# The first modulation of a two-layer transformer kernel: condition vector loaded first and turned alone, first four weight blocks split along the contraction

## The chip, the cores and the metric

The kernel runs on one core of one Trainium2 chip. The time is the device time of one execution, in microseconds (us); all numbers of a trace are counted from the start of its span. Engines are named as the profile names them: PE (TensorE), PEld (its weight loads), DVE (VectorE), ACT (ScalarE), POOL (GpSimd), SP (SyncE, which here only issues DMAs).

## The reference, cut to what matters

```
def reference(x, c, rel_bias, ada_w, ada_b, norm_attn, ...):       # x (1,512,1024), c (1,1024), all float32
    c_act = jax.nn.silu(c)
    for layer in range(2):
        mod = c_act @ ada_w[layer] + ada_b[layer]                    # ada_w[layer] (1024, 6144)
        sh_a, sc_a, g_a, sh_f, sc_f, g_f = jnp.split(mod, 6, axis=-1)
        h = modulate(rmsnorm(x, norm_attn[layer]), sh_a, sc_a)       # h * (1 + sc_a) + sh_a
        y = diff_attention(h, ...) if layer == 0 else dilated_attention(h, ...)
        x = x + g_a[:, None, :] * y
        h = modulate(rmsnorm(x, norm_ffn[layer]), sh_f, sc_f)
        x = x + g_f[:, None, :] * hier_moe(h, ...)
    return x
```

What matters here is the very first thing that layer 0 needs: `sh_a` and `sc_a`, the first 2048 columns of `c_act @ ada_w[0] + ada_b[0]`, and the normalised `x`, from which the modulated `h` is made for the first projections.

## The kernel before

Layer 0 is: setup, modulation, projections with attention between them, output projection, routing, then 32 experts whose weights are streamed; layer 1 the same with another attention. Each engine has its own instruction list in `program`, written out by hand, and the lists meet through semaphores. The order on an engine is the order of its code, and a waiting instruction holds all that stands behind it.

**Weights.** SP loads weights into a `ring` of six slots of 2 MB (`load`, L449, and L486 for the key and query weights, two halves of 1 MB) in the order that `block_order` gives: modulation blocks 0 to 3 ("mod 0" to "mod 3" below, slots 0 to 3), key and query weights of the first heads ("kq 0", slot 4), value weights ("v 0", slot 5), mod 4, 5, 6, kq 1, and so on. A slot is loaded again when its user is done (`used`). A modulation block before is 512 columns of `ada_w` with all 1024 rows, 8 pieces of 2 KB in each of 128 partitions. Tokens `x` come by a DMA of POOL (L558, 4 KB rows), followed on its queue by six small loads (L566). The constants and the small vectors come by ACT's DMAs (L684 to L702): constants, then `c`, norm gains and biases into rows of `W`, then the buckets of the position bias.

**Setup.** PE turns the vectors into columns (`colV` with 57 columns, `c` among them, L1607; `colA`, the modulation bias, L1608). DVE copies them from PSUM (L1020, L1026), scales a few and forms the sums for the mixing weight (L1028, L1030). ACT takes the Silu of `c` (L704) and the Exp for the mixing weight (L707), each with a table load. DVE spreads the result over 32 equal columns (L1033), so that PE can use it as weights. Two matmuls make the table of the position bias (L1611, L1612); DVE copies it (L1042, L1043), POOL writes it to DRAM (L568) and reads it back as a band matrix into `V` (L572, "hankel", which waits for kq 0 too).

**Norm.** ACT squares the four token chunks with a running sum (L732) and takes roots (L716); DVE normalises them into `XN` (L1052, L1056, L1060) and signals `xn_ready`.

**The first modulation.** For each of mod 0 to 3, PE multiplies the block (L1636): its four 32-column parts of the array work side by side on four of the eight contraction chunks, twice, so the 512 results stand in four partial sums of 32 equal rows. ACT copies them (L746); `mod_reduce` sums them over the partitions and turns them into a column, 4 matmuls with one column each (L1624); DVE adds the bias (`mod_columns`, L1100). After the fourth, DVE makes the scales (L1071) and signals `mod_ready`.

**The turn.** PE turns the normalised tokens, 8 groups of 4 transposes (L1670), into banks 2 to 5; ACT (L750, even groups) and DVE (L1115, odd groups) apply scale and shift while they copy to `HT`. A bank is used again when it has been copied.

**Projections.** `unit(n)`, 24 of them (L1695), two PSUM banks in turn. Unit 0 is the key of head 0, unit 1 its query. Behind unit 1 PE makes the bias tables (L1765, waits for the hankel DMA) and the reduction of mod 4 (L1624, again `mod_reduce`). From mod 4 on, DVE forms the modulation itself (`sum_part`, L1078 and L1080, 8 instructions for a block); in its list mod 4 stands ahead of copying out unit 0 (L1130), for which unit 2 waits.

Of the kernel before, what the change touches and what calls it, by code (L numbers as in the profile page):

```python
# [10 lines left out]
ALU = mybir.AluOpType  # L11
# [4 lines left out]
P = 128  # L16
# [25 lines left out]
C_KCOL, C_NCOL, C_SEL, C_END = 772, 773, 774, 810  # L42
# [3 lines left out]
V_C, V_NA, V_KN, V_KAB = 0, 8, 24, 32  # L46
V_QG, V_KG, V_SUB, V_BQ, V_BK = 48, 49, 50, 51, 54
V_END = 57
# [121 lines left out]
def constants():  # L170
# [14 lines left out]
    c[:, C_32] = 1 / 32  # L185
# [40 lines left out]
def program(nc, t, const, masks, buckets, out):  # L226
    with ExitStack() as ctx:
# [85 lines left out]
        t1_in, t1_pe, t1_copy = sem("t1_in"), sem("t1_pe"), sem("t1_copy")  # L313

# [106 lines left out]
        def _(sp):  # L421
# [129 lines left out]
            sp.wait_ge(out_done, 16 * TC)  # L551
# [130 lines left out]
        def _(act):  # L682

            act.dma_start(C[:, :], const).then_inc(const_in, 16)  # L684
            vecs = [(V_C, t["c"].rearrange("b (k p) -> (b k) p", p=P)),
                    (V_NA, t["norm_attn"].rearrange("l (k p) -> (l k) p", p=P)),
# [16 lines left out]
            act.wait_ge(setup_dve, 1)  # L703
            act.activation(cact[:, :], colV[:, V_C:V_C + KC], ACT.Silu).then_inc(setup_act, 1)  # L704

            act.wait_ge(setup_dve, 3)
            act.activation(lamw[:, 2:4], lamw[:, 0:2], ACT.Exp).then_inc(setup_act, 1)  # L707

            for l in range(LAYERS):
# [31 lines left out]
                if l == 0:  # L741
                    for i in range(4):
                        act.wait_ge(mod_pe, i + 1)
                        if i >= 2:
                            act.wait_ge(mod_red, i - 1)
                        act.activation(ACC[i % 2], bank[4 + i % 2], ACT.Identity).then_inc(mod_part, 1)  # L746
                    act.wait_ge(mod_ready, 1)
                    for k in range(0, KC, 2):
                        act.wait_ge(*s["xt_pe"](k + 1))
                        act.activation(ht3[:, k, :], bank[2 + k % 4], ACT.Identity,  # L750
                                       bias=mod[:, k:k + 1], scale=scl[:, 0, k:k + 1]).then_inc(s["ht_ready"].sem, 2)
# [51 lines left out]
                    act.add_instruction(mybir.InstLoadActFuncSet(name=nc.get_next_instruction_name(), act_func_set_id=LN_EXP_SET))  # L803
                    for n in range(UNITS0 + 6):
# [155 lines left out]
                if l == 0:  # L960
                    act.wait_ge(t1_pe, 1)
# [54 lines left out]
        def _(dve):  # L1016
            step = Steps(dve, dve_s)

            dve.wait_ge(setup_pe, 1)
            dve.tensor_copy(colV[:, :], bank[0][:, 0:V_END]).then_inc(setup_dve, 1)  # L1020
            dve.wait_ge(setup_dve, 1)
            step(dve.tensor_scalar(colV[:, V_QG:V_QG + 1], colV[:, V_QG:V_QG + 1], DH ** -0.5, None, ALU.mult))
            step(dve.tensor_scalar(colV[:, V_BQ:V_BQ + GROUPS], colV[:, V_BQ:V_BQ + GROUPS], DH ** -0.5, None, ALU.mult))
            step(dve.tensor_scalar(colV[:, V_SUB:V_SUB + 1], colV[:, V_SUB:V_SUB + 1], 1 - LAM_INIT, None, ALU.mult))
            dve.wait_ge(setup_pe, 2)
            dve.tensor_copy(colA[:, :], bank[1][:, 0:96]).then_inc(setup_dve, 1)  # L1026
            lp = W[:, 256:512].rearrange("p (a i n) -> p a i n", a=2, i=2)
# [7 lines left out]
            dve.wait_ge(setup_act, 2)  # L1035
            step(dve.tensor_tensor(lamw[:, 4:5], lamw[:, 3:4], lamw[:, 2:3], ALU.subtract))
            step(dve.tensor_scalar(nlam[:, :], lamw[:, 4:5], LAM_INIT, None, ALU.subtract))

            dve.wait_ge(bias_in, 32)
            dve.memset(V[BUCKETS:BUCKETS + 1, 4096 + FALL:4096 + FALL + H], NEG).then_inc(setup_dve, 1)  # L1040
            dve.wait_ge(setup_pe, 3)
            step(dve.tensor_copy(W[0:H, 0:512], bank[2][0:H, :]))  # L1042
            dve.tensor_copy(W[0:H, 512:512 + 3 * P], bank[3][0:H, 0:3 * P]).then_inc(setup_dve, 1)  # L1043

            for l in range(LAYERS):
# [60 lines left out]
                if l == 0:  # L1106
                    norm(s["ss_ready"], s["rms_arg"], s["rms_root"], s["xn_ready"])
                    for i in range(4):
                        mod_columns(i)
# [3 lines left out]
                    for k in range(1, KC, 2):  # L1113
                        dve.wait_ge(*s["xt_pe"](k + 1))
                        dve.tensor_scalar(ht3[:, k, :], bank[2 + k % 4], scl[:, 0, k:k + 1], mod[:, k:k + 1], ALU.mult, ALU.add).then_inc(q_ht, 1)  # L1115
# [487 lines left out]
        def _(pe):  # L1603

            pe.wait_ge(const_in, 16)
# [8 lines left out]
            def mod_reduce(i):  # L1614

                acc = ACC[i % 2]
                if i < 4:
                    pe.wait_ge(mod_part, i + 1)
                else:
                    pe.wait_ge(mod_sum, i - 3)  # L1620
                pe.wait_ge(mod_col, i)
                for j in range(4):
                    by_two = slice(2 * P * (j // 2) + j % 2, 2 * P * (j // 2 + 1), 2)
                    ins = pe.matmul(bank[6][:, 4 * i + j:4 * i + j + 1], acc[:, by_two if 6 <= i < 10 else slice(j * P, (j + 1) * P)],  # L1624
                                    C[:, C_32:C_32 + 1] if i < 4 else ones[:, 0:1], start=True, stop=True)
# [656 lines left out]
```

## Time and profile before

| | us |
|---|---|
| three runs | 1897.32, 1898.48, 1899.91; median 1898.48 |
| the profiled execution, device time | 1904.66 |
| its span in the trace | 1902.9 |
| PE busy | 1518.0 (80%) |
| DVE, ACT, POOL busy | 514.1, 371.6, 91.6 |
| DMA moved | 548.02 MB, mean 288 GB/s |

The page shows the span in 40 slices of 47.6 us with the busy share of each engine in tenths, and the chain of work that ended last by engine and line. The other views used are: the chain in order of time; the waits of one engine; the timeline (start, duration, line, shape, count, and in brackets the idle time of the engine before it with what ended it); windows (busy time of each engine in a stretch, and the granted clock of TensorE); and the DMA queues in a window. q1 is SP's queue, q10 ACT's, q0 POOL's.

### The profile page before, as it was taken

The page shows a single profiled execution, that of the slowest core. Times are in us where ns is not written, and L with a number is a line of the kernel's source. Part 1 is how long each engine was busy: PE and PEld are TensorE (multiplying, and loading weights), DVE is VectorE, ACT ScalarE, POOL GpSimd, SP SyncE. Part 2 cuts the span into 40 slices and gives each one's busy share as a digit, 9 for nine tenths or more (in the row PEclk, how much of TensorE's full clock was granted, in tenths as well). Part 3 has the DMA queues.
Part 4 walks back from the last instruction along what each step waited for, and adds up shares of the span by engine and source line. Part 5 has one row for each costly group of instructions (what it writes and reads, how often), then busy time and mean ns, then how long its engine had stood idle before and what let it go on. Part 6 is the DMA issues. An engine that isn't in the chain of part 4 may idle for free.

```text
span 1902.9 us, 16563 instructions
## 1 busy us (share of the span) xinstructions
PE 1518.0 (80%) x6360; PEld 671.8 (35%) x6360; DVE 514.1 (27%) x1178; ACT 371.6 (20%) x916; POOL 91.6 (5%) x99
## 2 busy tenths in 40 slices
PE   5999998997867757683698999998887756847845
PEld 2455554443222222231344455543432212312311
DVE  2675554340000000010576122225500100100103
ACT  3133344311101100110310234342210100101100
POOL 1000001010000000000000000002000000000000
PEclk9999998999878888897799999999998978978977
DMA  9972523389999999999766021021599999999996
GB/s 346 360 283 76 190 89 136 127 320 382 410 410 401 408 410 392 404 410 400 262 221 221 0 85 48 26 108 56 223 409 409 410 409 409 410 404 404 410 404 236
DMA packets 183413, 548.02 MB, mean 288 GB/s; under 512 B 8940, under 2 KB 46301, under 8 KB 182302
## 3 DMA queue, kind: packets, MB, share of 16 engines
q1 hardware_dynamic: 153536, 492.85, 66.5%
q0 software_dynamic: 12384, 36.41, 5.0%
q10 hardware_dynamic: 17406, 17.59, 2.9%
q8 instruction: 56, 0.92, 0.2%
q14 instruction: 31, 0.25, 0.0%
HBM read 530.37 MB, written 28.34 MB: 294 GB/s over the span
## 4 chain that ended last, share of the span: by engine, by line
PE 55%; DMA 27%; SPq 10%; DVE 5%; issue 2%; ACT 1%; DVEq 0%
PE psum L2144 12%; DMA ring<-in_moe_w_up_dram 11%; SPq L449 9%; PE psum L1897 9%; PE psum L1695 9%; DMA ring<-in_moe_w_down_dram 7%; PE psum L2177 5%; DMA ring<-in_moe_w_gate_dram 5%; PE psum L1867 3%; PE psum L1750 3%; DVE W L1080 1%; DMA T<-in_moe_w_up_dram 1%; DMA XN<-in_moe_w_up_dram 1%; DMA ring<-in_ada_w_dram 1%; PE psum L1724 1%
## 5 line engine op out<-in xcount | busy, mean ns | idle before, releaser
L2144 PE MATMUL psum<-ring,V 128*32 128x512 f32 (+2 forms) x1712 | 440.1, 677 | 182.1 <-DMA ring<-in_moe_w_up_dram 77.5
L2144 PEld LDWEIGHTS psum<-ring,V 128*32 128x32 f32 (+2 forms) x1712 | 145.2, 146 | 415.0 <-issue 408.5
L2177 PE MATMUL psum<-ring,V 128*32 128x512 f32 (+2 forms) x768 | 199.4, 661 | 74.0 <-DMA ring<-in_moe_w_down_dram 52.9
L975 ACT ACTIVATE V<-psum,modall,scls 128x128 f32<-128x128 f32 x216 | 81.3, 457 | 499.8 <-PE psum L2122 499.8
L1080 DVE SCALAR_TENSOR_TENSOR W<-ring,cact,W 128x512 f32<-128x512 f32 (+1 forms) x224 | 138.5, 618 | 7.7
L2144 PE MATMUL psum<-XN,V 128*32 128x512 f32 (+1 forms) x208 | 112.0, 700 | 23.0 <-DMA ring<-in_moe_w_gate_dram 15.2
L1494 DVE TENSOR_TENSOR V<-V,psum 128x512 f32<-128x512 f32 x28 | 19.3, 688 | 403.7 <-PE psum L2144 403.7
L2177 PEld LDWEIGHTS psum<-ring,V 128*32 128x32 f32 (+2 forms) x768 | 61.1, 141 | 168.8 <-issue 168.8
L1695 PE MATMUL psum<-HT,ring 128*128 128x512 f32 x256 | 115.4, 597 | 0.0
L2177 PE MATMUL psum<-XN,V 128*32 128x512 f32 (+2 forms) x192 | 101.4, 680 | 13.0 <-DMA ring<-in_moe_w_down_dram 13.0
L1510 DVE SCALAR_TENSOR_TENSOR HT<-psum,slot_gate,W 128x512 f32<-128x512 f32 x56 | 42.1, 751 | 255.1 <-PE psum L2177 255.1
L1897 PE MATMUL psum<-HT,ring 128*128 128x512 f32 x192 | 90.0, 614 | 0.0
L984 ACT ACTIVATE V<-psum 128x512 f32<-128x512 f32 x28 | 16.7, 597 | 366.2 <-PE psum L2144 366.2
L1897 PE MATMUL psum<-ring 128*128 128x512 f32 x192 | 87.0, 596 | 0.0
L1500 DVE COPY V<-psum 128x512 f32<-128x512 f32 x28 | 19.4, 692 | 239.7 <-PE psum L2155 239.7
L2144 PE MATMUL psum<-T,V 128*32 128x512 f32 (+2 forms) x128 | 67.3, 686 | 13.5 <-DMA ring<-in_moe_w_up_dram 13.5
L1695 PEld LDWEIGHTS psum<-HT,ring 128*128 128x128 f32 x256 | 47.5, 190 | 55.2 <-issue 54.6
L632 POOL DMA_INDIRECT expert_rows<-HT,dst x26 | 26.2, 1009 | 830.6 <-DVE HT L1510 830.6
L1695 PE MATMUL psum<-ring,HT 128*128 128x512 f32 x128 | 57.3, 597 | 0.0
L1867 PE MATMUL psum<-ring 128*128 128x512 f32 x128 | 56.9, 597 | 0.0
L1238 DVE SCALAR_TENSOR_TENSOR ring<-psum,colV,W 128x512 f32<-128x512 f32 x24 | 23.7, 989 | 113.7 <-ACT W L863 113.7
L1897 PEld LDWEIGHTS psum<-HT,ring 128*128 128x128 f32 x192 | 36.8, 196 | 44.8 <-issue 44.4
(311 smaller groups left out, 1656.8 us busy)
## 6 DMA issues: line engine op xcount, KB each, us to landing
ring<-in_moe_w_up_dram SPq DMA_DIRECT2D x54, 2048.0 KB, 24.2
ring<-in_moe_w_gate_dram SPq DMA_DIRECT2D x53, 2048.0 KB, 23.5
ring<-in_moe_w_down_dram SPq DMA_DIRECT2D x48, 2048.0 KB, 22.9
ring<-in_ada_w_dram SPq DMA_DIRECT2D x16, 2048.0 KB, 15.6
XN<-in_moe_w_down_dram SPq DMA_DIRECT2D x12, 2048.0 KB, 22.9
ring<-in_ada_w_dram ACTq DMA_DIRECT2D x16, 1024.0 KB, 5.3
XN<-in_moe_w_gate_dram SPq DMA_DIRECT2D x7, 2048.0 KB, 25.8
XN<-in_moe_w_up_dram SPq DMA_DIRECT2D x6, 2048.0 KB, 19.3
```

The source lines that it names most:

```text
L449: sp.dma_start(slot3(n, k), src).then_inc(w_in[SLOT[n]], 16)
L632: pool.indirect_dma_start(ys_d[l], bass.IndirectOffsetOnAxis(ap=rows, axis=0), HT[:, b * D:(b + 1) * D], None, bounds_check=last_row, oob_ ...
L975: ins = act.activation(V[:, 2 * D + b * D + k * P:2 * D + b * D + (k + 1) * P], bank[0][:, q * P:(q + 1) * P], ACT.Identity, bias=mod[:, 2 ...
L1080: ins = dve.scalar_tensor_tensor(acc, w[:, k, :], cact[:, k:k + 1], acc, ALU.mult, ALU.add)
L1238: dve.scalar_tensor_tensor(to, a, colV[:, gain:gain + 1], b, ALU.mult, ALU.mult).then_inc(s["qk_t"].sem, 1)
L1510: dve.scalar_tensor_tensor(HT[:, to], bank[6 + hf], slot_gate[:, COLS[p]:COLS[p] + 1], gf_row[:, hf * HALF:(hf + 1) * HALF], ALU.mult, ALU ...
L1695: ins = pe.matmul(bank[n % 2], rows, cols, start=(k == 0), stop=(k == KC - 1))
L1750: ins = pe.matmul(bank[WO_BANKS[0][u]], OT0[k][:, c * P:(c + 1) * P], w3[:, k, :], start=(k == 0), stop=(k == KC - 1))
L1867: ins = pe.matmul(bank[u % 4], rows, slot3(n)[:, k, :], start=(k == 0), stop=(k == KC - 1))
L1897: ins = pe.matmul(bank[n % 2], w[:, k, (hp % 2) * P:(hp % 2 + 1) * P], (HTQ if kind else ht3)[:, k, :], start=(k == 0), stop=(k == KC - 1))
L2144: ins = pe.matmul(bank[2 + 2 * i + b][half * w:(half + 1) * w, :], V[:, col:col + w], slot3(x)[:, k, :], start=(k == 0), stop=(k == KC - 1))
L2177: ins = pe.matmul(bank[6 + hf][half * w:(half + 1) * w, :], V[:, col:col + w], slot3(x, 4)[:, k, hf * HALF:(hf + 1) * HALF], start=(k == 0 ...
```

## The change

Modulation blocks 0 to 3 are no longer 512 columns with all rows, but 256 rows with all 2048 columns: 2 pieces of 8 KB in each partition in place of 8 of 2 KB. Each array part takes 512 of the columns, and all four blocks add into one bank; the sum is complete only after the fourth. ACT then copies once, 4 matmuls with 4 columns each reduce it (a constant table of 4 columns picks the array part), and DVE adds the bias once. The condition vector is ACT's first DMA, as 8 rows of its own, and PE turns it alone into bank 7; ACT takes the Silu from there, DVE spreads it, and mod 0 and mod 1 follow on PE ahead of the other vectors. DVE norms the tokens ahead of the vectors; PE turns the first four groups of tokens between mod 2 and mod 3, into banks 5, 7, 2, 3, with two matmuls on constants behind them whose result is not used. The Exp for the mixing weight stands behind the modulation, after the table load that the attention needs anyway.

```diff
-V_C, V_NA, V_KN, V_KAB = 0, 8, 24, 32
+V_NA, V_KN, V_KAB = 0, 16, 24
...
-    c[:, C_32] = 1 / 32
+    c[:, C_32:C_32 + 4] = (p // 32 == np.arange(4)[None, :]) / 32
...
+        c_in, c_turned = out_done, t1_pe
+        c_rows = W[0:KC, 1024:1024 + P]
...
-                    if kind == "mod":
+                    if kind == "mod" and i < 4:
+                        load(n, t["ada_w"][0][2 * P * i:2 * P * (i + 1), 0:4 * HALF].rearrange("(k p) n -> p k n", p=P), k=2)
+                    elif kind == "mod":
...
+            act.dma_start(c_rows, t["c"].rearrange("b (k p) -> (b k) p", p=P)).then_inc(c_in, 16)
             act.dma_start(C[:, :], const).then_inc(const_in, 16)
-            vecs = [(V_C, t["c"].rearrange("b (k p) -> (b k) p", p=P)),
...
-            act.wait_ge(setup_dve, 1)
-            act.activation(cact[:, :], colV[:, V_C:V_C + KC], ACT.Silu).then_inc(setup_act, 1)
-
-            act.wait_ge(setup_dve, 3)
-            act.activation(lamw[:, 2:4], lamw[:, 0:2], ACT.Exp).then_inc(setup_act, 1)
+            act.wait_ge(c_turned, 1)
+            act.activation(cact[:, :], bank[7][:, 0:KC], ACT.Silu).then_inc(setup_act, 1)
...
-                    for i in range(4):
-                        act.wait_ge(mod_pe, i + 1)
-                        if i >= 2:
-                            act.wait_ge(mod_red, i - 1)
-                        act.activation(ACC[i % 2], bank[4 + i % 2], ACT.Identity).then_inc(mod_part, 1)
+                    act.wait_ge(mod_pe, 4)
+                    act.activation(ACC[0], bank[4], ACT.Identity).then_inc(mod_part, 1)
...
+                    act.wait_ge(setup_dve, 4)
+                    act.activation(lamw[:, 2:4], lamw[:, 0:2], ACT.Exp).then_inc(setup_act, 1)
...
                 if l == 0:
                     norm(s["ss_ready"], s["rms_arg"], s["rms_root"], s["xn_ready"])
-                    for i in range(4):
-                        mod_columns(i)
+                    vectors()
+                    dve.wait_ge(mod_red, 4)
+                    dve.tensor_tensor(modall[:, 0:16], bank[6][:, 0:16], colA[:, 0:16], ALU.add).then_inc(mod_col, 4)
                     dve.wait_ge(mod_col, 4)
...
+            def mod_rows(i):
+                n = AT["mod", 0, i]
+                arrived(pe, n)
+                for k in range(2):
+                    for q in range(4):
+                        at = 2048 + 32 * (2 * i + k)
+                        ins = pe.matmul(bank[4][32 * q:32 * (q + 1), :], W[:, at:at + 32],
+                                        slot3(n, 2)[:, k, q * HALF:(q + 1) * HALF], start=(i == 0 and k == 0), stop=(i == 3 and k == 1))
+                ins.then_inc(mod_pe, 1)
+
+            pe.wait_ge(const_in, 16)
+            pe.wait_ge(c_in, 16)
+            pe.transpose(bank[7][:, 0:KC], c_rows, ident[0:KC, 0:KC]).then_inc(c_turned, 1)
+            pe.wait_ge(setup_dve, 1)
+            mod_rows(0)
+            mod_rows(1)
             pe.wait_ge(const_in, 16)
             pe.wait_ge(vec_in, 16 * N_VEC)
...
-            for i in range(4):
-                n = AT["mod", 0, i]
-                arrived(pe, n)
-                if i >= 2:
-                    pe.wait_ge(mod_part, i - 1)
...
-                if i:
-                    mod_reduce(i - 1)
-            mod_reduce(3)
...
+            mod_rows(2)
+            pe.wait_ge(*sm[0]["xn_ready"](TC))
+            pe.wait_ge(setup_dve, 6)
+            first_turns(range(4))
+            for _ in range(2):
+                pe.matmul(bank[0], ones, C[:, 0:512], start=True, stop=True)
+            mod_rows(3)
+            pe.wait_ge(mod_part, 1)
+            for j in range(4):
+                ins = pe.matmul(bank[6][:, j:16:4], ACC[0][:, j * P:(j + 1) * P], C[:, C_32:C_32 + 4], start=True, stop=True)
+            ins.then_inc(mod_red, 4)
...
+TURN0_BANKS = (5, 7, 2, 3)
```

`vectors()` is a new function of DVE's list that holds the old setup work (the copies of the turned vectors, the small scalings, the sums for the mixing weight, the copies of the bias table), with the same instructions as before. `first_turns` issues the groups of transposes that `xt_pe` counts; groups 4 to 7 stand where all eight stood. The difference of the two exponentials moves behind the copies to `HT` on DVE.

PE's list from its start to the first projections, before (`C` holds the constants, `W` the vectors and the spread `c`, `V` the bias table, `XN` the normalised tokens; `w_in0` to `w_in3` are the arrivals of mod 0 to 3, `w_in4` that of kq 0):

```order
L1607 MATMUL psum<-C,W 128x57 [waits vec_in,const_in]
L1608 MATMUL psum<-C,W 128x96
L1611 MATMUL psum<-V 8x512 [waits setup_dve]
L1612 MATMUL psum<-V 8x384
L1636 MATMUL psum<-ring,W 32x512 [waits w_in0]
L1636 MATMUL psum<-ring,W 32x512 x7
L1636 MATMUL psum<-ring,W 32x512 [waits w_in1]
...
L1636 MATMUL psum<-ring,W 32x512 [waits mod_part,w_in3]
...
L1670 MATMUL psum<-C,XN 128x128 [waits setup_dve,xn_ready]
...
L1695 MATMUL psum<-HT,ring 128x512 [waits ht_ready,w_in4]
```

The same stretch of the changed kernel:

```order
L1622 MATMUL psum<-C,W 128x8 [waits out_done,const_in]
L1616 MATMUL psum<-ring,W 32x512 [waits w_in0,setup_dve]
L1616 MATMUL psum<-ring,W 32x512 [waits w_in1]
...
L1628 MATMUL psum<-C,W 128x49 [waits vec_in,const_in]
L1629 MATMUL psum<-C,W 128x96
L1632 MATMUL psum<-V 8x512 [waits setup_dve]
L1633 MATMUL psum<-V 8x384
L1616 MATMUL psum<-ring,W 32x512 [waits w_in2]
...
L1649 MATMUL psum<-C,XN 128x128 [waits setup_dve,xn_ready]
L1649 MATMUL psum<-C,XN 128x128 x15
L1657 MATMUL psum<-C 128x512 x2
L1616 MATMUL psum<-ring,W 32x512 [waits w_in3]
```

The bias-table matmuls (L1611 before, L1632 now) stand behind mod 0 and 1 and ahead of mod 2, the first sixteen transposes ahead of mod 3.

DVE's list of the changed kernel, from its start to the scales:

```order
L1020 COPY W<-cact 128x256 [waits setup_act]
L1055 TENSOR_SCALAR small<-small 128x1 [waits ss_ready] x2
...
L1059 RECIPROCAL small<-small 128x1 [waits rms_root]
L1063 TENSOR_SCALAR XN<-X,small 128x1024 [waits dve_step]
L1025 COPY colV<-psum 128x49 [waits setup_pe]
...
L1038 MEMSET V 1x8 [waits bias_in]
L1040 COPY W<-psum 8x512 [waits setup_pe]
L1041 COPY W<-psum 8x384 [waits dve_step]
L1113 TENSOR_TENSOR modall<-psum,colA 128x16 [waits mod_red]
L1074 SCALAR_TENSOR_TENSOR scls<-modall,colV 128x8 [waits mod_col]
```

Before, the copies of `colV` and `colA` and the memset stood first, ahead of all four token chunks; now they stand behind the last. PE's bias-table matmuls wait for that memset (`setup_dve` 5).

## Rows read from the trace of the kernel before

**Rows 1.** The page: PE and DMA, busy tenths in 40 slices.
```profile
PE   5999998997867757683698999998887756847845
DMA  9972523389999999999766021021599999999996
```
**Rows 2.** The chain in order of time, 0 to 45: start, us, what.
```profile
12.66 22.27 DMA ring<-in_ada_w_dram
34.98 1.92 PE psum L1636 x16
...
39.25 5.22 PE psum L1670 x32
44.47 8.59 PE psum L1695 x20
```
**Rows 3.** Waits of PE, 0 to 300: total, times, longest.
```profile
PE psum L1733 <- DVE W L1142: 3.7, 1, 3.7
```
**Rows 4.** Timeline of setup and norm, 18 to 30.
```profile
19.22 0.22 DVE L1020 COPY colV<-psum 128x57 f32<-128x57 f32 x1 [19.22 <-PE psum L1607]
...
20.54 0.29 DVE L1030 TENSOR_REDUCE lamw<-W 128x2 f32<-128x128 f32 x1
...
21.10 1.04 ACT L732 ACTIVATE HT<-X 128x1024 f32<-128x1024 f32 x1
...
21.75 1.87 PE L1611 MATMUL psum<-V 33*8 33x512 f32 x2 [2.22 <-DVE V L1040]
...
26.30 0.20 ACT L716 ACTIVATE small<-small 128x1 f32<-128x1 f32 x1 [1.58 <-DVE small L1052]
...
29.91 0.75 DVE L1060 TENSOR_SCALAR XN<-X,small 128x1024 f32<-128x1024 f32 x1
```
**Rows 5.** The DMA of x (view of tile X, 0 to 45): its issue, its landing.
```profile
L558 POOL DMA_DIRECT2D X<-in_x_dram x1: 929/929/929, 1.3 to 1.3; - x1
...
DMA to landing us min/median/max: 15.0/15.0/15.0
```
**Rows 6.** DMA queues, 7 to 8 us: packets, MB, share of 16 engines.
```profile
q0 software_dynamic: 65, 0.27, 66.1%
q1 hardware_dynamic: 64, 0.13, 33.8%
```
**Rows 7.** DMA queues, 355 to 356 us, when rows of 8 KB are written.
```profile
q0 software_dynamic: 50, 0.41, 97.8%
```
**Rows 8.** Windows: stretch, PE, PEld, DVE, ACT, POOL busy (x), PEclk, DMA, GB/s.
```profile
24.84:29.07 4.23, 4.23 (x21) 0.98 (x24) 3.60 (x12) 2.65 (x9) 0.55 (x1) 1.00 1.05 387
29.07:32.50 3.43, 3.43 (x36) 1.63 (x32) 1.72 (x4) 1.16 (x3) 0.00 (x0) 1.00 1.05 388
39.30:42.70 3.40, 3.40 (x18) 3.40 (x17) 1.17 (x4) 1.56 (x2) 0.93 (x1) 0.50 1.07 381
42.70:44.40 1.70, 1.70 (x17) 1.70 (x16) 1.54 (x2) 1.05 (x2) 0.00 (x0) 1.00 1.03 381
```
**Rows 9.** Timeline from the last modulation block to the first copies.
```profile
36.97 0.60 ACT L746 ACTIVATE W<-psum 128x512 f32<-128x512 f32 x1 [2.92 <-PE psum L1636]
...
38.23 1.02 PE L1624 MATMUL psum<-C,W 128*128 128x1 f32 x8 [0.35 <-DVE modall L1100]
...
39.48 0.17 DVE L1071 SCALAR_TENSOR_TENSOR scls<-modall,colV 128x8 f32<-128x8 f32 x1
...
40.18 0.78 ACT L750 ACTIVATE HT<-psum,modall,scls 128x512 f32<-128x512 f32 x1 [2.62 <-PE psum L1670]
```
**Rows 10.** Timeline, the landings of kq 0 and mod 4, and what follows.
```profile
41.49 0.93 POOL L572 DMA_DIRECT2D V<-bias_scratch  x1 [14.45 <-DMA ring<-in_a_w_qkv_dram]
...
57.97 0.49 DVE L1078 TENSOR_SCALAR W<-ring,cact 128x512 f32<-128x512 f32 x1 [12.65 <-DMA ring<-in_ada_w_dram]
...
63.89 0.75 DVE L1130 SCALAR_TENSOR_TENSOR X<-psum,colV,W 128x512 f32<-128x512 f32 x1
...
66.87 1.96 PE L1695 MATMUL psum<-ring,HT 128*128 128x512 f32 x4
```

More of the change, by code:

```diff
@@ L749, in _ @@
                         act.wait_ge(*s["xt_pe"](k + 1))
-                        act.activation(ht3[:, k, :], bank[2 + k % 4], ACT.Identity,
+                        act.activation(ht3[:, k, :], bank[TURN0_BANKS[k % 4]], ACT.Identity,
                                        bias=mod[:, k:k + 1], scale=scl[:, 0, k:k + 1]).then_inc(s["ht_ready"].sem, 2)
@@ L1042, in _, with vectors @@
-            step(dve.tensor_copy(W[0:H, 0:512], bank[2][0:H, :]))
-            dve.tensor_copy(W[0:H, 512:512 + 3 * P], bank[3][0:H, 0:3 * P]).then_inc(setup_dve, 1)
+            def vectors():
+                dve.wait_ge(setup_pe, 1)
+                dve.tensor_copy(colV[:, :], bank[0][:, 0:V_END]).then_inc(setup_dve, 1)
+                dve.wait_ge(setup_dve, 2)
+                step(dve.tensor_scalar(colV[:, V_QG:V_QG + 1], colV[:, V_QG:V_QG + 1], DH ** -0.5, None, ALU.mult))
+                step(dve.tensor_scalar(colV[:, V_BQ:V_BQ + GROUPS], colV[:, V_BQ:V_BQ + GROUPS], DH ** -0.5, None, ALU.mult))
+                step(dve.tensor_scalar(colV[:, V_SUB:V_SUB + 1], colV[:, V_SUB:V_SUB + 1], 1 - LAM_INIT, None, ALU.mult))
+                dve.wait_ge(setup_pe, 2)
+                dve.tensor_copy(colA[:, :], bank[1][:, 0:96]).then_inc(setup_dve, 1)
+                lp = W[:, 256:512].rearrange("p (a i n) -> p a i n", a=2, i=2)
+                step(dve.tensor_tensor(W[:, 512:640].rearrange("p (a n) -> p a n", a=2),
+                                       lp[:, :, 0, :], lp[:, :, 1, :], ALU.mult))
+                dve.tensor_reduce(lamw[:, 0:2], W[:, 512:640].rearrange("p (a n) -> p a n", a=2), AX.X,
+                                  ALU.add).then_inc(setup_dve, 1)
+                dve.wait_ge(bias_in, 32)
+                dve.memset(V[BUCKETS:BUCKETS + 1, 4096 + FALL:4096 + FALL + H], NEG).then_inc(setup_dve, 1)
+                dve.wait_ge(setup_pe, 3)
+                step(dve.tensor_copy(W[0:H, 0:512], bank[2][0:H, :]))
+                dve.tensor_copy(W[0:H, 512:512 + 3 * P], bank[3][0:H, 0:3 * P]).then_inc(setup_dve, 1)
@@ L1114, in _ @@
                         dve.wait_ge(*s["xt_pe"](k + 1))
-                        dve.tensor_scalar(ht3[:, k, :], bank[2 + k % 4], scl[:, 0, k:k + 1], mod[:, k:k + 1], ALU.mult, ALU.add).then_inc(q_ht, 1)
+                        dve.tensor_scalar(ht3[:, k, :], bank[TURN0_BANKS[k % 4]], scl[:, 0, k:k + 1], mod[:, k:k + 1], ALU.mult, ALU.add).then_inc(q_ht, 1)
+                    mix_weight()
                     def unit_out(n):
@@ L1616, in mod_reduce @@
                 acc = ACC[i % 2]
[L1617 to L1620, printed above, removed]
+                pe.wait_ge(mod_sum, i - 3)
                 pe.wait_ge(mod_col, i)
@@ L1661, in turned_in @@
                             pe.wait_ge(*s["ht_ready"](k + 1))
-                    pe.wait_ge(*s["xn_ready"](TC))
-                    for k in range(KC):
-                        if k >= 4:
-                            turned_in(k - 4)
-                        elif k < 2:
-                            pe.wait_ge(setup_dve, 6)
-                        for c in range(TC):
-                            ins = pe.transpose(bank[2 + k % 4][:, c * P:(c + 1) * P], xn3[:, c, k * P:(k + 1) * P], ident)
-                        ins.then_inc(s["xt_pe"].sem, 1)
+                    for k in range(4, KC):
+                        turned_in(k - 4)
+                        first_turns(range(k, k + 1))
                     def unit(n):
```

50 lines of the change are left out of this document (17 added, 33 removed).

## The prediction

> **What bounds the kernel now.** I read the slices of the page first, then the chain in order of time over the start, then the timeline of the same stretch. The slices [rows 1] show the core starting slowly on PE (5, then 9s up to the sixth) while DMA is full for two slices: the weights and x come in together. The chain [rows 2] says what ends last: mod 3, issued at 12.66, lands at 34.93; its matmuls end at 36.9; the turn of the tokens follows from 39.25 to 44.47; then unit 0. From there PE stands still only once up to 300 us for longer than a fraction, 3.7 us for DVE [rows 3], and DVE is there behind PE's own scores. So the start of unit 0, now 44.3, moves nearly the whole program: projections, routing and the expert stream wait for each other from there, and I let a shift of unit 0 pass one to one to the end.
>
> Two limits stand close behind. Kq 0 lands at 41.4, when POOL's hankel read is let go [rows 10]. Mod 4 lands at 57.97; DVE sums it, then copies unit 0 out, done at 64.6, while PE starts unit 2 at 66.87 [rows 10]: 2.2 us of slack.
>
> **What goes.** Four waits for a reduction become one. Each `mod_reduce` is 1.02 us of PE [rows 9], three of them go. Behind mod 3 the way to the scales was 36.9 to 39.65 (L1071, 39.48 and 0.17) [rows 9] and becomes: copy 0.60, four matmuls 1.02, add 0.16, scales 0.17, and about 0.25 of steps between, 2.2 us: 0.5 less. Half of the turn is done before; what is left behind the scales is one copy (0.78 [rows 9]) and four groups of four transposes, at the fast pace 0.1 us each (17 matmuls in 1.7 us, against 18 in 3.4 at half clock [rows 8]): 2.5 us, where 4.7 passed from scales to unit 0 before. If nothing else moved, unit 0 would come 2.7 us earlier.
>
> The blocks themselves load a little faster. A packet of 8 KB takes 0.313 us (97.8% of 16 engines in a us, for 50 packets [rows 7]), 410 GB/s, where 2 KB pieces run at 388 [rows 8]: four blocks of 2.1 MB in 20.5 in place of 21.6 us, 1.1 earlier for mod 3, kq 0 (40.3) and mod 4. The lone `c`, the Silu and the spreading are done near 10 us and free mod 0 and mod 1 from the vectors, which land near 19 [rows 4]; PE would be idle then. The Exp, its table load and the mixing weight now stand behind the copies to `HT`; DVE's sum of mod 4 is queued behind them, but its data is missing until 57 anyway, so nothing. C is issued half a us later behind `c`; PE needs it only for mod 0. SP's last wait is longer by a DMA long landed.
>
> **What comes: x.** In the window 7 to 8 us, q0 (x, 4 KB) and q1 (the blocks, 2 KB) moved 65 and 64 packets [rows 6]: the engines take them in turn, packet for packet, whatever their size. A packet of x costs 0.163 us, one of the blocks 0.084 [rows 6]. With 8 KB the second becomes 0.313. x is 512 packets, 32 for each engine, so it is later by 32 x 0.229 = 7.3 us: landing at 16.3 [rows 5] becomes 23.6. The blocks gain what x loses. The page "DMA: Bandwidth & Descriptors" of the Trainium skill, section on queues, rings and completion order, says the same against this change: an engine goes round its queues at packet granularity and drains a whole packet before it switches. The trace agrees (65 to 64); no row shows SP's queue with 8 KB.
>
> Before, ACT squared the first chunk only at 21.10, because it was held by the vectors and the Exp [rows 4], so 2.5 of the 7.3 us count. The norm took from 21.10 to 30.66, of which ACT stood 1.58 us at the first root for a DVE busy with the bias table [rows 4]; that goes. So `xn_ready` is full at 23.6 + 9.56 - 1.58 = 31.6, 0.9 later than before.
>
> **What comes: a chain behind the norm.** Before, the vectors and the bias table were done by 26.3, when the first root was let go [rows 4], under the loads. Now DVE does them behind the last chunk, and PE has mod 2, the turn and mod 3 queued behind the bias-table matmuls, which wait for DVE's memset. In us:
> - vectors on DVE up to the memset: 19.22 to 20.83 before, and 0.1: 1.7, so 33.3.
> - bias-table matmuls, 21.75 to 24.84 before [rows 4, 8], on a PE that has been idle since mod 1 and the vectors: 3.1, so 36.4. At full clock it would be 1.5.
> - mod 2, landed by then: half clock 3.4 (the first 21 matmuls took 4.23), full clock 1.7 (16 of the 36 in 3.43) [rows 8].
> - 16 transposes: 3.0 or 1.6 [rows 8]; the copies of the bias table (1.3) hide beside mod 2.
> - the two unused matmuls, each four passes over 512 columns, as long together as a block of mod: 1.7. They are there for the clock; they are on this chain.
> - mod 3, landed since 34: 1.7.
> These four are 6.7 us at full clock. Before, the pace rose at 29.07, 4.2 us after the first block began at 24.84, though PE had worked since 21.75 [rows 4, 8] (that window's PEclk says 1.00, as no level was on record yet; 21 matmuls against 36 say 1.2 GHz against 2.4). I take the same 4.2 us at half clock, which cost 2.1. Mod 3 then ends at 36.4 + 6.7 + 2.1 = 45.2, the scales at 47.4, unit 0 starts at 47.4 + 2.5 = 49.9, against 44.3: **5.6 us later**. No landing binds then; mod 4 is early for DVE.
>
> The bounds of the open costs. The clock: PE warm from the first matmul on gives 1.5 + 2.1 less, so +2.0; cold up to mod 3, or a fall to 1.2 GHz in the turn as at 39.3 before [rows 8], 1.3 to 2 more, +7.5. The packets: between x as before (nothing added; it could not be served better than with 2 KB beside it) and 7.3; I take 7.3, since an 8 KB packet is on record in this trace as one [rows 7] and the sharing by count is too [rows 6].
>
> The sum is made against the profiled execution (span 1902.9, 1904.66 us); the median of the runs is 6 us under it. I carry the difference over: 1898.5 + 5.6 = 1904.1, 0.3%. About 0.2%, 3.8 us, is what a measurement of this kernel can tell from no change.
>
> **The rivals.**
> 1. *An 8 KB row goes as two 4 KB packets.* Then a round grows by 0.163 - 0.084 = 0.08 us, x lands at 18.8, all behind it 4.8 earlier: +0.8, 1899.3, no change to be told. For: POOL's x, rows of 4 KB, is sent so, and so far nothing larger was seen on q1. Against: rows 7. In its section on SWDGE the same page says that a packet is preferably at most 4096 B; by that rule this rival would hold on POOL's queue, and there [rows 7] the trace disagrees.
> 2. *The other side: x is not late.* If the sharing under load isn't by count, x lands at 16.3 and ACT begins there; all behind is 7.3 earlier: 49.9 becomes 42.6, -1.7, 1896.8. With a warm clock on top (-3.6) unit 0 would stand at 39.0; kq 0's landing (40.3) holds it, -4.0, and mod 4 with its 2.2 us of slack and 1.1 earlier allows -3.3 behind unit 1: 1895.2. This is the place and the price: the way from x to the norm, decided by x landing before about 18. For it: the shorter ends above are real, and PE and DMA have room. Against: the equal counts. It would have to go further than its own limits to be over 0.2% faster, so I give that little, for what my sum leaves out.
> 3. *The shift is lost on the way.* Later slack (DVE in the units, the DMA stream of the experts) takes most of it: within 2 us of before. For: the 3.7 us wait [rows 3]. Against: that wait is behind PE's own work, and the expert stream starts with the routing.
>
> **How the numbers follow.** The late x 0.57, of which a warm clock leaves a fifth under 3.8 us; two packets 0.17; x in time 0.18; lost on the way 0.08. Slower by over 0.2%: 0.8 x 0.57 = 0.46, and 0.01 for costs not seen (the first rival with a cold clock is +2.7, not enough): 0.47. Faster by over 0.2%: only from the second rival and from what is not seen, 0.12. The rest, 0.41, is within. The predicted time is the likeliest case, 1904. The range: its upper end is the cold clock, 1898.5 + 7.5 = 1906; the lower end takes in the first rival and the cold end of the second, 1896. The likeliest case alone has 1900.5 to 1906.
>
> **What would show it.** The landing of x near 23.6 and about 32 packets a us of q0 beside as many 8 KB packets of q1. `xn_ready` (the last L1063) ending near 31.6. The bias-table matmuls (L1632) starting near 33.3, released by DVE, after PE's long gap. Mod 3 (L1616) not waiting for its DMA. The scales (L1074) near 47.4 and unit 0 (L1710) near 50 at 2.4 GHz. I am wrong if x lands before 19, if L1632 starts before 30, or if the last chain still runs through the landing of mod 3.

## The result, and the profile after

The changed kernel took 1911.16 us (median of 4 runs, 1909.09 to 1911.66) against 1899.2 us for the kernel before (4 runs, 1897.32 to 1902.19): 1.0059 times the time, 95% interval 1.0042 to 1.0077. Slower, as forecast, but above the top of the range (1906). The profiled execution took 1909.09 us, its span is 1907.3.

The timeline of the changed kernel, from the landing of the constants to unit 0 (start, duration, engine and line, shape, count, and in brackets the idle time before with what ended it):

```profile
10.96 0.27 PE L1622 MATMUL psum<-C,W 8*128 8x8 f32 x1 [10.96 <-DMA C<-in_const_dram]
11.82 3.64 PE L1616 MATMUL psum<-ring,W 128*32 128x512 f32 x16 [0.59 <-DVE W L1020]
18.66 3.64 PE L1616 MATMUL psum<-ring,W 128*32 128x512 f32 x16 [3.20 <-DMA ring<-in_ada_w_dram]
23.94 1.06 ACT L733 ACTIVATE HT<-X 128x1024 f32<-128x1024 f32 x1 [12.50 <-DMA X<-in_x_dram]
...
31.19 0.76 DVE L1063 TENSOR_SCALAR XN<-X,small 128x1024 f32<-128x1024 f32 x1
...
32.62 0.31 PE L1628 MATMUL psum<-C,W 49*128 49x49 f32 x1 [10.32 <-DMA V<-in_masks_dram]
...
32.97 0.21 DVE L1025 COPY colV<-psum 128x49 f32<-128x49 f32 x1 [1.03 <-PE psum L1628]
...
34.63 0.07 DVE L1038 MEMSET V<- 1x8 f32 x1
...
34.75 1.87 PE L1632 MATMUL psum<-V 33*8 33x512 f32 x2 [1.46 <-DVE V L1038]
...
36.41 1.48 PE L1633 MATMUL psum<-V 33*8 33x384 f32 x2
...
37.83 3.61 PE L1616 MATMUL psum<-ring,W 128*32 128x512 f32 x16
...
41.36 1.97 PE L1649 MATMUL psum<-C,XN 128*128 128x128 f32 x16
...
43.16 1.88 PE L1657 MATMUL psum<-C 128*128 128x512 f32 x4
...
44.98 1.92 PE L1616 MATMUL psum<-ring,W 128*32 128x512 f32 x16
...
46.97 0.60 ACT L744 ACTIVATE W<-psum 128x512 f32<-128x512 f32 x1 [16.54 <-PE psum L1616]
...
48.99 0.17 DVE L1074 SCALAR_TENSOR_TENSOR scls<-modall,colV 128x8 f32<-128x8 f32 x1
...
50.08 1.97 PE L1649 MATMUL psum<-C,XN 128*128 128x128 f32 x16 [1.40 <-ACT HT L748]
...
51.88 8.75 PE L1710 MATMUL psum<-HT,ring 128*128 128x512 f32 x20
```

In the kernel before, unit 0 reads:

```profile
44.31 8.75 PE L1695 MATMUL psum<-HT,ring 128*128 128x512 f32 x20
```

Read against [rows 4, 9]. ACT squares the first chunk at 23.94 in place of 21.10, released by x. The last chunk is normalised at 31.95, 1.3 later than before. Then comes what the prediction did not have: PE turns the vectors only at 32.62, released by a DMA called `V<-in_masks_dram`, 10.3 us after its last work. Everything behind that is the predicted chain: memset, bias table, mod 2, transposes, two unused matmuls, mod 3, scales, unit 0, with PE waiting for no weights. The pace doubles at 41.36: mod 2 takes 3.6 us for 16 matmuls, mod 3 takes 1.92 for the same 16. Unit 0 starts at 51.88; before it was 44.31 (the chain of [rows 2] counts it from 44.47): **7.6 us later**.

The chain of work that ended last says the same (0 to 60, start, us, what): the chain no longer goes through mod 3 [rows 2] but through the flip matrix (`V<-in_masks_dram`), the last small load of ACT's queue that PE's turn of the vectors counts, and from the bias table on through PE alone up to mod 3.

```profile
7.62 24.87 DMA V<-in_masks_dram
34.75 1.87 PE psum L1632 x2
36.62 1.28 PE psum L1633 x2
37.90 3.54 PE psum L1616 x16
41.43 1.90 PE psum L1649 x16
43.33 1.72 PE psum L1657 x4
45.05 1.90 PE psum L1616 x16
```

The DMA from issue to landing of x (tile X), and the queues in the window 12 to 13 us (packets, MB, share of 16 engines). They answer to [rows 5, 6].

```profile
DMA to landing us min/median/max: 22.6/22.6/22.6
```
```profile
q1 hardware_dynamic: 33, 0.27, 65.9%
q0 software_dynamic: 33, 0.14, 33.4%
q10 hardware_dynamic: 35, 0.01, 4.5%
```

Three queues, three nearly equal counts: 33 packets of 8 KB (0.27 MB) from SP, 33 of 4 KB from POOL, 35 small ones from ACT. x and ACT's small loads both pay for the large packets of the blocks. The page "DMA: Bandwidth & Descriptors" of the Trainium skill (queues, rings and completion order) has the engines go round their queues packet by packet, and the trace agrees with these counts.

### The profile page after: what moved, and what is told of

Read it like the earlier page. It is cut to its first block, busy times and chain, and to the rows that moved or that the text cites. A ratio compares the mean times of both kernels' runs of the same rounds, so it can differ in the third digit from the quotient of the medians.

```text
span 1907.3 us, 16512 instructions
## 1 busy us (share of the span) xinstructions
PE 1518.6 (80%) x6341; PEld 667.2 (35%) x6341; DVE 513.7 (27%) x1175; ACT 368.5 (19%) x912; POOL 91.4 (5%) x99
## 4 chain that ended last, share of the span: by engine, by line
PE 55%; DMA 27%; SPq 9%; DVE 5%; issue 2%; ACT 1%; ACTq 0%; DVEq 0%
DMA ring<-in_moe_w_up_dram 11%; PE psum L2159 11%; PE psum L1912 9%; PE psum L1710 9%; SPq L451 8%; DMA ring<-in_moe_w_down_dram 7%; PE psum L2192 6%; DMA ring<-in_moe_w_gate_dram 5%; PE psum L1882 3%; PE psum L1765 3%; DMA V<-in_masks_dram 1%; DVE W L1083 1%; DMA T<-in_moe_w_up_dram 1%; PE psum L2017 1%; PE psum L1739 1%
```

## The experiments

Below, "unit 0" is the start of its matmuls in the run's trace, given also as the difference from 44.31 before. "Ratio" is against runs of the kernel before on the same chip. All diffs are against the changed kernel, unless another is named.

**1. The changed kernel again** (`p8k`, and `again8k` on another chip), no edit.

> The changed kernel as it is, beside the kernel before on the same chip. Theory A (the late x and the late vectors, then a chain on DVE and PE behind the norm): the shift at unit 0 (7.6 us in the one trace of each so far, 51.9 against 44.3) goes to the end nearly unchanged, so the ratio is 1.0035 to 1.0045. Theory B (something beyond the start also costs, since the medians stood 12 us apart): 1.006 and more.

> The changed kernel once more, on whatever chip this call gets. Theory A: the shift is the start's 7.6 to 8.3 us of unit 0 in every trace, and what the medians say (12 us, then 5.9) is the spread between chips and executions; the ratio is again between 1.002 and 1.006. Rival (a cost elsewhere that one chip shows and another not): over 1.006, with anchors behind the routing that lie further from the kernel before than unit 0 does.

`p8k`: 1907.07 against 1901.51 us, ratio 1.0031 (1.0019 to 1.0043), unit 0 at 52.6 (+8.3). `again8k`: 1907.82 against 1901.33, 1.0035 (1.0023 to 1.0048), unit 0 at 52.1 (+7.8). Slower three times out of three, though by less than at first. The start repeats: x is squared at 23.97 in `p8k` and 23.88 in `again8k`, the vectors are turned at 32.81 and 32.57, all within 0.2 us of the first trace.

**2. The size of a piece.** Each of blocks 0 to 3 is loaded in 2 DMAs with rows of 4 KB (`p4k`, shown) or in 4 with rows of 2 KB (`p2k`), the same bytes to the same place:

```diff
-                        load(n, ...)
+                        slot_free(n)
+                        rows = t["ada_w"][0][2 * P * i:2 * P * (i + 1), 0:4 * HALF].rearrange("(k p) n -> p k n", p=P)
+                        for j in range(2):
+                            sp.dma_start(slot3(n, 2)[:, :, 1024 * j:1024 * (j + 1)], rows[:, :, 1024 * j:1024 * (j + 1)]).then_inc(w_in[SLOT[n]], 16)
```

> The same four row blocks, each loaded by two DMAs of 1024 columns, so SP's queue carries packets of 4 KB. Theory A with packets served in turns: x lands near 18.7 (22.6 + 1.3 = 23.9 with 8 KB), the flip matrix near 25 (32.5 with 8 KB), the last normalisation ends near 26.7, the bias-table matmuls start near 28.5, unit 0 near 45.5; time 5 to 6 us under the 8 KB version, about as the kernel before. Rival (the size of the pieces does not matter, the order of the work alone costs): unit 0 at 51.9 as with 8 KB and the same time.

> The same four row blocks, each loaded by four DMAs of 512 columns: packets of 2 KB as in the kernel before, all else as in the change. Theory A: x lands near 16.3, the flip matrix near 19, the last normalisation ends near 24.3, the bias-table matmuls start near 26, unit 0 near 42.5, 1.8 us before the kernel before; time 8 to 10 us under the 8 KB version, ratio 0.999. Rival (order alone costs): unit 0 later than 48, ratio over 1.003.

`p4k`: 1903.11 us, 1.0007 (0.9995 to 1.002), unit 0 at 48.1 (+3.8). `p2k`: 1902.74, 1.0004 (0.9991 to 1.0016), unit 0 at 45.1 (+0.8). So 8, 4 and 2 KB give +8.3, +3.8 and +0.8: the size of a piece, and nothing else that was edited (but the number of DMAs that cut it), makes 7.5 us at unit 0. In the time it makes 4.3 (1907.07 to 1902.74). The queues of `p4k`, 12 to 13 us, are in turn again, now with equal bytes:

```profile
q1 hardware_dynamic: 48, 0.20, 49.1%
q0 software_dynamic: 48, 0.20, 48.2%
q10 hardware_dynamic: 47, 0.02, 6.9%
```

My price for `p4k` missed by as much as x did: x was squared at 21.21, 2.4 later than the 18.8 of rival 1, which this run builds (why is open), and unit 0 came 2.6 later than the 45.5 expected. The norm still comes last, but only just: in the timeline of `p4k` mod 1 waits for its landing, the vectors stand behind it on PE, and they are turned 0.8 us before the last chunk is normalised at 29.21.

```profile
25.19 3.30 PE L1619 MATMUL psum<-ring,W 128*32 128x512 f32 x16 [9.03 <-DMA ring<-in_ada_w_dram]
...
28.43 0.26 PE L1631 MATMUL psum<-C,W 49*128 49x49 f32 x1
28.46 0.75 DVE L1066 TENSOR_SCALAR XN<-X,small 128x1024 f32<-128x1024 f32 x1
...
30.90 1.38 PE L1635 MATMUL psum<-V 33*8 33x512 f32 x2 [1.98 <-DVE V L1041]
```

In `p2k` it is PE that comes last: x is squared at 16.04 and normalised by 24.1, but mod 1, landed at 24.18, ends at 27.4, the vectors are turned at 27.36, and the bias table starts at 29.52 where it began at 21.75 before. Even with x in time the new order gains nothing here, since mod 1 stands ahead of the vectors.

**3. x out of the race** (`x_first`): 8 KB rows kept, but x is SP's first DMA.

```diff
+            sp.dma_start(x3, t["x"][0].rearrange("(c p) n -> p c n", p=P)).then_inc(x_in, 16)
             for l in range(LAYERS):
...
-            pool.dma_start(x3, t["x"][0].rearrange("(c p) n -> p c n", p=P)).then_inc(x_in, 16)
```

> 8 KB pieces as in the change, but x is SP's first DMA and not POOL's, so it does not share turns with the blocks behind it. Theory A: x lands near 8, the norm is over by 17, the vectors on ACT's queue land some us earlier than 32.5 because POOL's big packets no longer take turns (26 to 28), and are now the last thing waited for; unit 0 near 44 to 46. If the vectors' landing stays at 32.5, unit 0 stays near 51, and it is they and not x that bind. Rival (order alone costs): unit 0 at 51.9.

1901.58 us, 0.9998 (0.9989 to 1.0007), unit 0 at 46.2 (+1.9). x is squared at 11.85, and in the time no loss is left to see. What remains at unit 0 is the chain of experiment 2: mod 1 from 23.30 (after a wait for its landing), the vectors behind it, the bias table at 29.02.

```profile
26.86 0.34 PE L1628 MATMUL psum<-C,W 49*128 49x49 f32 x1
```

PE no longer waits for the vectors here: they too have landed, 5.6 us and more ahead of the 32.49 of the changed kernel. So this edit moved both late loads, as the smaller pieces did, and neither run says what x alone is worth.

**4. The small load that held the vectors** (`noflip8k`): the flip matrix (`V<-in_masks_dram`) was counted among the vectors, though the bias tables behind unit 1 alone read it. It gets a semaphore of its own.

```diff
-flip, masks[:, M_FLIP:M_FLIP + P]).then_inc(vec_in, 16)
+flip, masks[:, M_FLIP:M_FLIP + P]).then_inc(flip_in, 16)
...
+                            pe.wait_ge(flip_in, 16)
```

> The changed kernel, but the turns of the vectors no longer wait for the flip matrix, which is the last of the DMAs counted there and is used only behind unit 1 (it has a semaphore of its own). Theory A: the vectors ahead of it land near 28, so DVE starts on them right behind the norm at 32.0 and not at 33.0: unit 0 1 us earlier, time the same within what can be told. Rival (the whole queue is late, not its last matrix): PE's wait ends at 32 again.

1907.15 us, 1.0029 (1.0016 to 1.0042), unit 0 at 50.9 (+6.6), against +7.6 to +8.3. PE turns the vectors at 29.70, and now it is the norm and the next small load that hold the memset:

```profile
29.70 0.31 PE L1629 MATMUL psum<-C,W 49*128 49x49 f32 x1 [7.22 <-DMA W<-in_a_lambda_dram]
...
33.39 0.07 DVE L1039 MEMSET V<- 1x8 f32 x1 [0.31 <-DMA V<-in_rel_bias_dram]
```

Unit 0 is 0.9 to 1.7 us earlier than in the three traces of the changed kernel, as the theory says (in this trace the norm ended at 31.57, 0.4 earlier than in the first one, and that is part of it); in the time, the interval overlaps that of the change itself.

**5. The unused matmuls left out** (`no_dummy`):

```diff
-            for _ in range(2):
-                pe.matmul(bank[0], ones, C[:, 0:512], start=True, stop=True)
```

> The change without its two unused matmuls. Theory A: they only lengthen the chain, since mod 3 has long landed and PE has no gap to bridge: unit 0 1.8 us earlier, time 1.8 us lower, the granted clock still full from mod 3 to unit 0. Rival (they hold the clock): the granted clock falls to 0.5 in or behind mod 3, unit 0 no earlier or later.

1908.67 us, 1.0037 (1.0024 to 1.005), unit 0 at 52.0 (+7.7): nothing gained. The first turns take 2.86 us, against 1.97 in the changed kernel, so the scales come at 48.17, only 0.8 earlier, and the last turns then slow down. Its timeline and its windows (the columns as in [rows 8]):

```profile
49.26 2.94 PE L1649 MATMUL psum<-C,XN 128*128 128x128 f32 x16 [1.40 <-ACT HT L748]
```
```profile
49.26:50.00 0.74, 0.74 (x7) 0.74 (x8) 0.64 (x1) 0.61 (x1) 0.00 (x0) 1.00 1.02 385
50.20:51.90 1.70, 1.70 (x10) 1.70 (x9) 0.81 (x1) 1.05 (x2) 0.00 (x0) 0.50 1.03 387
```

The granted clock goes from 1.00 to 0.50 amid the turns, and 16 matmuls take 2.94 in place of 1.97 us. So the 1.8 us of the two matmuls are lost again, one half ahead of mod 3 and the other behind it. Their absence can't be the reason for the first half, since the first turns stand ahead of their place, and for the second it is not shown: `again8k`, with both matmuls and on the same chip, loses the clock in the same turns.

```profile
49.58 2.79 PE L1649 MATMUL psum<-C,XN 128*128 128x128 f32 x16 [1.40 <-ACT HT L748]
```

**6. PE kept at work in its gaps** (`warm8k`): nine unused matmuls of 512 columns behind mod 1 and two ahead of the bias table.

```diff
             mod_rows(1)
+            pe.matmul(bank[7][:, 0:512], ones, C[:, 0:512], start=True, stop=True)
...
+            pe.matmul(bank[7][:, 0:384], ones, C[:, 0:384], start=True, stop=True)
             pe.wait_ge(setup_dve, 5)
```

> The changed kernel with unused matmuls on constants in PE's gaps (nine between mod 1 and the vectors, two while it waits for DVE's memset), so that PE is at 2.4 GHz when the chain behind the norm begins. Theory A: the bias-table matmuls take 1.5 us and not 3.1, mod 2 1.8 and not 3.6, unit 0 3 to 3.5 us earlier than in the change (51.9 to 52.6), time 3 us lower. Rival (pace is not what the chain waits for, DVE and the landings are): unit 0 moves by less than 1 us.

Unit 0 at 50.3 (+6.0), 1.6 to 2.3 earlier than in the change and not 3 to 3.5; 1911.48 us, 1.0055 (1.0034 to 1.0076). The mechanism held at its place: the bias table takes 1.6 us in place of 3.1, mod 2 1.92 in place of 3.61, the scales come at 45.8, 3.2 earlier. Half of it goes again in the last turns (3.61 us for 16, granted clock 0.50 from 46.9 to 50.3). The time missed: it did not fall. Its four runs are two near 1908.5 (mean granted clock 0.900 and 0.901) and two near 1914.4 (0.896); this run settles the half-clock stretch, not the time.

**7. x first, and the vectors ahead of mod 1** (`xo8` with 8 KB rows, `xo4` with the 4 KB pieces of experiment 2): both with x as in `x_first`; PE's order is mod 0, vectors and bias table, mod 1, the turns, mod 2, the unused matmuls, mod 3.

```diff
-            mod_rows(1)
             pe.wait_ge(const_in, 16)
             pe.wait_ge(vec_in, 16 * N_VEC)
...
-            mod_rows(2)
+            mod_rows(1)
             pe.wait_ge(*sm[0]["xn_ready"](TC))
...
             first_turns(range(4))
+            mod_rows(2)
```

> x as SP's first DMA, 8 KB pieces, and PE's list in the order mod 0, vectors and bias table, mod 1, first turns, mod 2, unused matmuls, mod 3. With x first alone unit 0 stood at 46.2 although x was normed by 19.9: PE did mod 1, the bias table, mod 2 and the turns in one cold row behind mod 1's landing. Theory A: the vectors land near 26 by the turns of the queues, the bias table then runs 28 to 31, mod 1 and the rest behind it as before: unit 0 within 1 us of 46.2. If the vectors are there by 22, unit 0 near 42 and the time 3 us under the kernel before.

> The same with pieces of 4 KB. Theory A: the small vectors on ACT's queue wait half as long for each turn and land near 20, so the bias table is done by 26 and mod 3's landing (34 to 35) binds again: unit 0 at 41 to 42, 2.5 to 3 us before the kernel before; ratio 0.998 to 0.999. Rival (the pieces do not matter for the vectors): unit 0 as in the 8 KB version of this order.

`xo8`: 1905.07 us, 1.0023 (1.0014 to 1.0031), unit 0 at 50.0 (+5.7): worse than `x_first`. `xo4`: 1900.3, 0.9997 (0.9988 to 1.0005), unit 0 at 45.0 (+0.7). The rows of `xo8` show why:

```profile
17.24 3.64 PE L1616 MATMUL psum<-ring,W 128*32 128x512 f32 x16 [6.57 <-DMA ring<-in_ada_w_dram]
...
26.00 0.31 PE L1627 MATMUL psum<-C,W 49*128 49x49 f32 x1 [5.12 <-DMA V<-in_masks_dram]
...
28.53 0.07 DVE L1038 MEMSET V<- 1x8 f32 x1 [0.57 <-DMA V<-in_rel_bias_dram]
...
46.72 3.52 PE L1648 MATMUL psum<-C,XN 128*128 128x128 f32 x16 [1.40 <-ACT HT L748]
```

With 8 KB rows ACT's small loads are late even without x: the vectors land at 26.0, and mod 1, put behind them, waits with them, so the chain behind the bias table holds one block more. With 4 KB they are there when mod 0 ends (turned at 22.15). Both lose the clock in the last turns (3.52 and 3.39 us).

**8. A version to beat both** (`best_a`): `xo4`, with the unused matmuls where PE waits anyway: none ahead of mod 3, 384 columns while ACT copies the sum, 512 and 256 while the scales and the first copy are made. `best_b` adds more of them: five ahead of mod 0, one ahead of the bias table, three ahead of mod 3. `best_a` against `xo4`:

```diff
-            for _ in range(2):
-                pe.matmul(bank[0], ones, C[:, 0:512], start=True, stop=True)
             mod_rows(3)
+            pe.matmul(bank[0][:, 0:384], ones, C[:, 0:384], start=True, stop=True)
             pe.wait_ge(mod_part, 1)
...
             ins.then_inc(mod_red, 4)
+            pe.matmul(bank[0][:, 0:512], ones, C[:, 0:512], start=True, stop=True)
+            pe.matmul(bank[0][:, 0:256], ones, C[:, 0:256], start=True, stop=True)
```

> The 4 KB version with x first and the new order on PE (unit 0 at 45.0), with the unused matmuls moved: none ahead of mod 3, one of 384 columns while ACT copies the sum, 768 columns while DVE and ACT make the first copy. In that version the clock fell to 1.2 GHz at 41.3, in the last turns. Theory A: the clock stays up, the last turns take 1.7 us and not 3.4, and mod 3 begins 1.9 earlier or when it lands: unit 0 at 41 to 41.5, 3 us before the kernel before, ratio 0.9985. Rival: the clock falls all the same, unit 0 near 43.

> The same with unused matmuls also ahead of mod 0, ahead of the bias table and ahead of mod 3, so PE never cools from 12 us on. Theory A: mod 3's landing (34 to 35) binds, unit 0 at 40.5 to 41, no better than the version before by more than 0.7 us, since the landings of mod 3 and kq 0 are the same. Rival (the cold stretch still cost there): 2 us better.

`best_a`: 1895.85 us (12 runs, 1891.49 to 1899.97) against 1902.25, ratio **0.997 (0.9959 to 0.9981)**, unit 0 at 41.16 (-3.2): faster than both kernels.

```profile
32.34 3.84 PE L1619 MATMUL psum<-ring,W 128*32 128x512 f32 x32
36.11 0.91 PE L1660 MATMUL psum<-C 128*128 128x384 f32 x2
36.24 0.60 ACT L747 ACTIVATE W<-psum 128x512 f32<-128x512 f32 x1 [18.00 <-PE psum L1619]
36.90 1.05 PE L1663 MATMUL psum<-C,W 128*128 128x4 f32 x8
37.81 1.10 PE L1665 MATMUL psum<-C 128*128 128x512 f32 x2
...
38.27 0.17 DVE L1077 SCALAR_TENSOR_TENSOR scls<-modall,colV 128x8 f32<-128x8 f32 x1
...
38.75 0.59 PE L1666 MATMUL psum<-C 128*128 128x256 f32 x2
39.36 1.97 PE L1651 MATMUL psum<-C,XN 128*128 128x128 f32 x16
41.16 8.75 PE L1714 MATMUL psum<-HT,ring 128*128 128x512 f32 x20
```

Mod 2 and mod 3 follow each other (32 in 3.84 us), PE stands nowhere long up to unit 0, and the last turns take 1.97. Of the 6.4 us in the median, the start explains the 3.2 of unit 0; the rest is not explained by anything edited. `best_b`: 1900.66 us, 0.9988 (0.9978 to 0.9999), unit 0 at 41.35 (-3.0). It is warm from the start, but mod 3 waits for its landing in both (its weight loads begin at 34.25 in `best_a`, at 34.45 there), so it cannot be earlier. Why it is 4.8 us behind `best_a` with the same unit 0 stays open; about 1 may go with the mean granted clock of its runs (0.903 against 0.904, medians 0.903 and 0.905, and the slope given below). The start is not where they part: POOL's load of x behind the projections (314.13 before) comes at 310.38 in `best_a` and at 308.29 in `best_b`, and only by the routing of layer 1 is `best_a` ahead.

## Why the prediction missed

**Right.** The packets in turn: x landing forecast at 23.6, measured 23.9, one packet of x for one of the blocks; the norm full at 31.6, measured 31.95; the chain behind it in the order given, with no block awaited, and 3.5 us of half clock inside (forecast 4.2). Rival 1 (two 4 KB packets) is out by the counts and bytes of the queues, rival 2 (x in time) by its landing, rival 3 (the shift is lost) by the times. That the large packets are the cause is shown from two sides: smaller pieces take the loss away in steps, and x ahead of them on their own queue takes it away in the time (1.0031 to 0.9998). That x alone is the cause, as I had it, is not shown, and the trace speaks against it: DVE's copy of the vectors (32.97) was released by their landing, so x in time with the vectors at 32.5 would have saved nothing at unit 0. Both loads were late, the norm behind x ended at 31.95 and the flip matrix landed at 32.49, and each hides the other.

**The step that failed** is "the vectors, which land near 19 [rows 4]", and with it "No landing binds then". I let x pay for the large packets and kept the landing of ACT's small loads from the trace of before, though that queue goes through the same turns: its last counted load needed 24.87 us from issue and landed at 32.5. The constants landed late as well, at 10.96. So the vectors came after the norm and not far ahead of it. In the sum this step is worth 0.9 us, and `noflip8k` gives 0.9 to 1.7 at unit 0.

**Term by term, to unit 0**, in us against the forecast:
- norm 31.95 in place of 31.6: +0.35
- vectors to memset: copy at 32.97, where the forecast had it 0.1 behind the norm: +0.9 for the flip matrix; bias table starting at 34.75, not 33.3, holds both and 0.2 of steps
- bias table 3.1: as said
- mod 2 to mod 3, 37.83 to 46.90: 9.1 in place of 8.8, +0.3. Two errors meet here: the half clock cost 1.7 (mod 2 in 3.6 for 1.9) and not 2.1, and the pieces at full clock take 1.8 (turns), 1.8 (unused) and 1.9 (each block), where I had 1.6, 1.7 and 1.7
- scales behind mod 3, 2.3 for 2.2: +0.1
- last turns, 49.16 to 51.88: 2.7 for 2.5, +0.2

Together 51.9 in place of 49.9, +7.6 in place of +5.6. One term made nearly half of that miss, the rest are terms that are 0.1 to 0.4 too small.

**From unit 0 to the end**, "pass one to one to the end" holds. In the two traces, POOL's load of x behind the projections moves from 314.13 to 322.22 (+8.1), and one of POOL's last scatters, in the experts of layer 1, from 1780.51 to 1788.81 (+8.3). Only the last 120 us give 3.9 back, and for another reason, given below. Over the twelve runs above, a straight line through the difference of the medians against the shift of unit 0 has slope 0.99 and offset -1.0 us, with 2 us of scatter (slope 0.86 without `best_a`): from -3.2 and -6.4 (`best_a`) to +8.3 and +5.6 (`p8k`). By it +7.6 at unit 0 gives about +6.6.

**The remaining 5 us.** The first comparison shows +12.0 between medians, two later ones +5.6 and +6.5. Here my account is weaker. Some 2 us lie in the kernel before: its median of four runs was 1899.2, those of the 25 to 33 runs of the later comparisons 1901.3 to 1902.3. The runs also differ in their mean granted clock, and the time goes with it: over 29 runs of the kernel before on one chip, a clock lower by 0.001 goes with 0.7 us more (correlation -0.82); on the two other chips it is 0.7 and 0.4 (-0.61 and -0.40). In the first comparison the changed kernel ran at 0.905 (1909.09 us) and three times at 0.895 to 0.898 (1911.1 to 1911.7); in `p8k` the median clock is 0.900, and its one run at 0.894 took 1913.2 us. That covers 1 to 2 us. One place where executions part is seen in the traces: the last 16 matmuls of the program (L2248 before, L2263 in the changed kernel) take 7.10 us in the changed kernel's, and 9.83 in the trace of before, at a granted clock of 0.72 and behind a wait of 3.73 in place of 1.73; 10.15 in `warm8k` and 9.94 in `best_b`, 7.11 in `best_a`. That is up to 4 us which the start has nothing to do with, and the 3.9 us above. Whether the changed start itself makes a lower clock later on was not tested, and what is left stays open. Against the later comparisons 1904 is 1.0029 of 1898.5, close to their 1.0031 and 1.0035; but that is two errors that meet, since unit 0 was 2 to 2.7 us later than I said.

**The range** was too narrow at the top for a reason of its own: +7.5 was the cold clock alone. A late landing on the third queue, and medians of three or four runs that lie 2 to 4 us from the later ones, had no place in it.

## What to carry to other kernels

When rows of one stream get longer, count what *every* queue has in flight beside it, small loads above all: here each of their packets paid one large packet (35 a us beside 33 of 8 KB), and a wait that counts all of them is as late as the last. Two loads that are late together hide each other, so move both before judging one. Put the first-needed tensor in front of the large rows on the same queue instead of letting it race them. If unused matmuls are to keep the clock up, put them where PE waits anyway: on the chain the two cost 1.8 us.

## What the runs showed of the hardware that I had not expected

- **A few small loads are slowed as much as a large one.** With 8 KB rows from SP the constants land at 10.96 and the flip matrix 24.87 us after its issue; with the 2 KB pieces of `p2k` the constants land at 8.04. (Before, as the first DMA of ACT's queue, they landed 4.0 us after their issue at 0.75; behind `c` in `p2k` it is 6.6 from 1.4. That costs nothing here.) In `xo8`, without x beside it on POOL's queue, the flip matrix still lands at 26.0.
- **The clock falls in the middle of work.** In `no_dummy`, `xo8`, `xo4`, `again8k` and `warm8k` it goes from 1.00 to 0.50 during or at the start of the last turns, though PE had just done mod 3 at full pace; between them lie the copy of the sum, eight small matmuls and the wait for the first copy to `HT`. `best_a` and `best_b`, with unused matmuls in these gaps, kept 1.00 through the turns. But the changed kernel kept it without them in two of three traces, and `p4k`, `p2k`, `x_first` and `noflip8k` did too (1.97 us for the 16): six of eleven traces without, two of two with. That the matmuls in the gaps hold the clock is likely, not shown.
- **A level that is not on record reads as 1.00.** The window 34.75 to 41.20 of the changed kernel gives a clock of 1.00, while mod 2 took 3.61 us for what took 1.92 at 44.98; the durations, not that column, show the half clock there.
